# A two-block network on one core: 512 KB weight blocks fetched as two transfers of 64 rows

## The reference, cut to what matters

```python
proj = x @ w_in                                         # first layer: 2048 -> 3136
q = (_rmsnorm(c_q, q_norm) @ w_qb)                      # 512 -> 3072
kv = (_rmsnorm(c_kv, kv_norm) @ w_kvb)                  # 512 -> 4096
return (attn * jax.nn.silu(z)) @ w_out                  # 2048 -> 2048
...
proj = x @ w_in                                         # second layer: 2048 -> 8208
return (hcell * jax.nn.silu(z)) @ w_out                 # 2048 -> 2048
...
mod = c_act @ w_ada[l] + b_ada[l]                       # 2048 -> 12288, one row
proj = h @ w_in[l]                                      # second block: 2048 -> 8704
merged = jax.nn.sigmoid(ga) * (ya @ w_oa[l]) + jax.nn.sigmoid(gb) * (yb @ w_ob[l])
x = x + g1 * (merged @ w_out[l])
ff = (jax.nn.silu(h2 @ w_ffn_gate[l]) * (h2 @ w_ffn_up[l])) @ w_ffn_down[l]
```

## Time and profile before

| | |
|---|---|
| median of 3 runs | 2185.49 us |
| the profiled execution | 2186.84 us |
| its span | 2185.2 us |
| mean granted TensorE clock | 0.998 |
| TensorE busy | 2158.7 us |
| DVE busy | 1522.9 us |
| ScalarE busy | 1025.5 us |
| POOL busy | 311.0 us |
| moved by DMA | 522.69 MB, mean 239 GB/s |

### The profile page before, as it was taken

One profiled execution on the slowest core, in us unless ns is written; L12 is line 12 of the kernel. 1 busy time (PEld: TensorE's weight loads), 2 busy tenths in 40 slices (PEclk: granted clock), 3 DMA queues, 4 the chain that ended last, 5 costly groups with the idle time before them and its releaser, 6 DMA issues.

```text
span 2185.2 us, 30129 instructions
## 1 busy us (share of the span) xinstructions
PE 2158.7 (99%) x10030; PEld 1798.1 (82%) x10030; DVE 1522.9 (70%) x2065; ACT 1025.5 (47%) x1255; POOL 311.0 (14%) x580
## 2 busy tenths in 40 slices
PE   9999999999999999999999999999999999999998
PEld 8898888777888887887888888888888888888886
DVE  6766668788677978597876768775666666554544
ACT  5445544356445446434555444454444444444433
POOL 2101111221110010701111211111111111000000
PEclk9999999999999999999999999999999999999999
DMA  8887577897987684969766887757888887775564
GB/s 294 246 221 254 174 266 246 245 301 233 302 278 208 188 306 143 268 222 297 255 190 198 295 268 239 242 205 251 262 259 277 266 262 240 223 231 186 191 196 139
DMA packets 206444, 522.69 MB, mean 239 GB/s; under 512 B 33104, under 2 KB 60400, under 8 KB 205424
## 3 DMA queue, kind: packets, MB, share of 16 engines
q1 hardware_dynamic: 166256, 394.10, 56.7%
q0 software_dynamic: 39776, 126.41, 18.1%
q10 hardware_dynamic: 288, 0.52, 0.1%
HBM read 507.82 MB, written 13.16 MB: 238 GB/s over the span
## 4 chain that ended last, share of the span: by engine, by line
PE 89%; DVE 4%; DMA 3%; ACT 2%; issue 1%; SPq 0%; DVEq 0%; ACTq 0%
PE ps L2424 81%; PE ps L2468 2%; DMA ada_raw<-in_w_ada_dram 1%; DVE lo L1360 1%; DVE acc_s L1372 1%; ACT hi L771 1%; DMA raw<-in_ml_w_in_dram 1%; PE ps L2521 1%; PE ps L2894 1%; PE ps L2883 1%; PE ps L2781 0%; DMA raw<-in_w_in_dram 0%; DVE conv_tmp L1854 0%; PE ps L2614 0%; PE ps L2615 0%
## 5 line engine op out<-in xcount | busy, mean ns | idle before, releaser
L1360 DVE TENSOR_TENSOR lo<-raw,hi 128x1024 fp32r<-128x1024 f32 x731 | 889.9, 1222 | 547.5 <-ACT hi L771 544.6
L771 ACT CAST hi<-raw 128x1024 fp32r<-128x1024 f32 x731 | 765.4, 1051 | 991.1 <-PE ps L2424 808.4
L2424 PE MATMUL ps<-hi,XH 128*128 128x512 f32 x2196 | 686.8, 393 | 9.6 <-DVE lo L1360 7.4
L2424 PE MATMUL ps<-lo,XH 128*128 128x512 f32 x2196 | 680.1, 390 | 0.0
L2424 PE MATMUL ps<-hi,XL 128*128 128x512 f32 x2196 | 679.5, 389 | 0.0
L2424 PEld LDWEIGHTS ps<-hi,XH 128*128 128x128 f32 x2196 | 408.8, 188 | 97.0 <-DVE lo L1360 12.5
L2424 PEld LDWEIGHTS ps<-lo,XH 128*128 128x128 f32 x2196 | 412.7, 188 | 86.7
L2424 PEld LDWEIGHTS ps<-hi,XL 128*128 128x128 f32 x2196 | 412.5, 188 | 86.6
L643 POOL DMA_DIRECT2D ada_raw<-in_w_ada_dram x224 | 120.3, 537 | 788.1 <-DVE acc_s L1372 512.0
L1372 DVE SCALAR_TENSOR_TENSOR acc_s<-ada_raw,c_act,acc_s 128x512 f32<-128x512 f32 x256 | 191.1, 746 | 34.0 <-DMA ada_raw<-in_w_ada_dram 32.8
L665 POOL DMA_DIRECT2D ada_raw<-in_w_ada_dram x160 | 86.4, 541 | 346.5 <-DVE acc_s L1372 194.9
(11 more groups left out here) (396 smaller groups left out, 1695.5 us busy)
## 6 DMA issues: line engine op xcount, KB each, us to landing
ada_raw<-in_w_ada_dram POOLq DMA_DIRECT2D x384, 256.0 KB, 5.0
raw<-in_w_in_dram SPq DMA_DIRECT2D x136, 512.0 KB, 4.7
raw<-in_ml_w_in_dram SPq DMA_DIRECT2D x128, 512.0 KB, 4.7
raw<-in_w_gate_dram SPq DMA_DIRECT2D x176, 256.0 KB, 3.0
raw<-in_w_up_dram SPq DMA_DIRECT2D x176, 256.0 KB, 3.5
raw<-in_w_down_dram SPq DMA_DIRECT2D x88, 512.0 KB, 4.4
raw<-in_mla_w_in_dram SPq DMA_DIRECT2D x47, 512.0 KB, 5.1
raw<-in_mla_w_out_dram SPq DMA_DIRECT2D x32, 512.0 KB, 4.9
```

Source lines behind the costliest of these rows:

```text
L771: nc.scalar.copy(hi[:, j, :], raw[:, j, :]).then_inc(hi_ready, 1)
L1360: nc.vector.tensor_tensor(lo[:, j, :], raw[:, j, :], hi[:, j, :].bitcast(F32), ALU.subtract) \
L2424: ins = mm(ps[:, o:o + HALF], x, w[:, b % RING, c0:c0 + HALF], start=first, stop=(k == n_rows - 1 and x is xl), skip_group_check=True)
```

## The change

From the second projection on, every transfer of a 512 KB block is issued as two, rows 0 to 63 and rows 64 to 127, each 256 KB, into the same slot and onto the same semaphore. The first 16 blocks and the gate and up blocks stay as they are. All blocks behind the first 16 now count two transfers, and the wait targets follow.

```diff
@@ landed
-            two = max(0, min(n + 1, B_DOWN) - B_FFN)
-            two = (two + RING - 1 - j) // RING if two > 0 else 0
-            return 16 * (n // RING + 1 + two)
+            return 16 * (n // RING + 1 + max(0, n // RING + 1 - KD // RING))
@@ stream
                         sp.wait_ge(lo_ready, n0 + RING * g + j - RING + 1)
-                        sp.dma_start(dst, src).then_inc(w_landed[j], 16)
+                        for half in (slice(0, P // 2), slice(P // 2, P)):
+                            sp.dma_start(dst[half], src[half]).then_inc(w_landed[j], 16)
@@ blocks
                     sp.wait_ge(lo_ready, n0 + b - RING + 1)
-                    sp.dma_start(*plain(w, c0)(b, b % RING)).then_inc(w_landed[b % RING], 16)
+                    dst, src = plain(w, c0)(b, b % RING)
+                    for half in (slice(0, P // 2), slice(P // 2, P)):
+                        sp.dma_start(dst[half], src[half]).then_inc(w_landed[b % RING], 16)
@@ rest
-                        hi_block(RING * g + (n0 + j), j, 16 * g + c0)
+                        hi_block(RING * g + (n0 + j), j, 32 * g + c0)
```

## The result

The change makes the kernel slower: 2344.47 us median of six runs (2341.09 to 2350.51) against 2184.93 us beside it, a ratio of 1.0727 with a 95% interval of 1.0715 to 1.0739. That is 159.5 us more. The forecast was 2237 us with a range up to 2305; the sign was right and so was the cause (each transfer writes one side of the partitions), but the 50 us of the sum are a third of what came.

A forecast was written before the change was run, and what follows sets the result against it. TensorE was taken as the bound, with DMA near a limit in the fullest stages. Halves at 218 GB/s lose 50 us over the listed stretches: 2186.84 + 50 = 2237 us, range 2183 to 2305.

The forecast's parts named there:

- the sum: Over six stretches, weight bytes at 218 GB/s, all others at 406, excess over each stretch's length lost: together 50 us.
- What bounds it: Whole kernel: TensorE, busy 2158.7 of 2185.2 us, is the bound; only 26.5 us of idle time could be won.
- Issues and waits cost nothing: SP's two issues per block (0.67 of 2.72 us) and ScalarE's wait for 32 increments cost nothing.
- The rate of a half: Weight transfers to 64 partitions go at 218 GB/s, the mean of four regroup stretches; all other traffic at 406.
- the six stretches: Windows 294-354, 403-549, 549-633, 958-1052, 1217-1440 and 1929-2163 us (down projection, no cost); together 50 us lost.
- The stages not listed have room: Stages outside the sum give more time to a block or have less traffic beside it, so no loss.
- The path of the loss: In new stalls `raw` lands late, then `hi`, `lo`, TensorE wait; `ada` accumulations and `ada_raw` loads follow; no size given.
- The clock: TensorE's clock drops after idle time: five to ten drops of 1.7 us, counted in "Slower by more".
- Slower by more: Also the deeper rival: halves at 190 GB/s or less, plus clock drops; some 2330 us, chance 0.14.
- No difference: Regroups slow from their scratch source, or engines out of step; halves at about 400 GB/s, 2186 us, chance 0.21.
- faster: Split blocks land earlier; half a microsecond off each of ten late blocks is 5 us: 2182 us, chance 0.07.
- The signs: 549 to 633 us: 3.1 us per block, 250 to 270 GB/s, landings 3 us later; down projection share over 0.9.

The follow-up runs named there:

- regroup run: The kernel before with each regroup's four loads over all 128 partitions, a quarter of the columns each: 2180.07 us against 2186.13, ratio 0.9972.

## Why the prediction was right or wrong

**What bounds it.** Right. TensorE was the bound with next to nothing to win, the stages near 300 GB/s were near a limit, and the change pushed them over it.

**Issues and waits cost nothing.** Right within 3 to 6 us where blocks are on time, by the runs with even and odd rows and with columns, where the same number of transfers came to 1.0027 and 1.0011. One issue of 64 rows takes SP 468 ns, though, and not the 333 of a whole block, so a block costs it 0.94 us and not 0.67. And where blocks are late, the idle time that was to cover this is gone: SP's issues are 2% of the chain of the changed kernel, some 37 us if its pieces are added up, where they were under 1 us. How much of that is net loss was not separated.

**The rate of a half, taken at 218 GB/s, and all other traffic at 406.** The direction was right, and the nearest rows were of the right kind, as the regroup run shows. For the 32-block stage split alone the size held: 220 GB/s in the terms of the sum, and 12.7 us where the sum had 14.5. In the change, with split stages on both sides, the same stage comes to 205 GB/s and lost 18.3. The sum is steep there, since a block has 2.72 us and asks for 193 GB/s: by the prediction's own working the six stretches lose 50 us at 218 and 82 at 205. They lost 11.4 (306.3 to 362.9 before), 19.8, 18.3, 16.6, 29.8 (1217.3 to 1453.0 before) and 0 (down projection), 96 us in all. So this term was mis-sized by a factor of two, of which the lower rate explains two thirds.

The packet times show what was wrong in its form. The sum slowed the weights alone and left everything else at 406 GB/s. In the 32-block stage `ada_raw` went at 258 and the halves at 237; in the run with even and odd rows, with as many and as large transfers, `ada_raw` went at 369 (8.28 MB in 26.7% of 84 us). A confined transfer thus holds up its neighbours nearly as much as it is slowed itself. Nor were the rows behind 218 a rate of confined transfers beside weights: in 427 to 430 and 152 to 156 us nearly all bytes were those of POOL's queue, regroup loads and `ada_raw`; in 484 to 488 and 984 to 989 weights of 128 rows were about half.

The Trainium skill's rule (SBUF — State Buffer, "Door 1: The DMA port swizzle") spoke against the change, and the runs agree with the rule. Its 196 GB/s gave an estimated 107 us for those stretches, nearer to the 96 measured than my 50. The prediction calls the regroup rows within a few per cent of that figure; they lie 7 to 17% above it, and the halves' packet times of 223 to 263 GB/s lie 14 to 34% above. So the figure did well as a term of this sum, but the halves are nowhere seen to run at it.

**The stages not listed have room.** This is the step that failed: "they have room" on the average was taken for "no loss". The rest of the span's 154.2 us, 58 us, lies in them: 15.6 in the mLSTM output projection, 13.3 between 850 and 958 us (now 941.5 to 1062.8), 7.5 in the query, key and value stage, 7.3 in the first convolution inputs (362.9 to 402.8 before). In two of them, the mLSTM output projection and the first convolution inputs, SP puts 512 KB row loads between the blocks, and an average over the stage hides them. In the convolution inputs TensorE was busy all of the 39.9 us before, with the engines 81% busy. In the change a block behind the row loads landed 13.7 us after its issue, while the ring covers four blocks of work, 10.9 us, and TensorE was idle for 4.8 us of 47.2. Splitting the mLSTM output projection alone cost all of its 15 us, and splitting its first 12 blocks nothing clear of the noise. For the 13.3 us between 850 and 958 us and the 7.5 us of the query, key and value stage, the cause stays open.

**The path of the loss.** The prediction has `raw` as what is late, and `ada_raw` only behind a late `lo`. Landings of `raw` are the larger part. But `ada_raw` was late by itself, and DVE waited for it ahead of a `lo` (79.6 us against 32.8). The sum had no term for this.

**The clock.** I gave it to the deeper rival. The mean granted clock fell from 0.998 to 0.984. It was at 0.50 in twelve stretches of 3.4 to 10.2 us, 68 us together, where the kernel before had one of 3.4. In the 5 us ahead of each of the twelve, TensorE was busy for 0.5 to 3.0 us only. One of them:

```profile
190.00:195.40 5.40, 1.64 (x8) 1.02 (x6) 3.65 (x4) 1.34 (x2) 0.55 (x2) 1.00 1.03 247
195.50:202.30 6.80, 3.49 (x10) 3.03 (x11) 2.38 (x7) 4.15 (x4) 1.07 (x2) 0.50 1.03 254
```

At 0.50, 1.2 GHz, it stayed for 6.8 us here, as the earlier trace rows have it for 3.4. In full-speed time that is an estimated 37.4 us (0.016 of 2339.4) against 4.4 before, 33 us more, and it may explain most of the 48 us of added busy time. The 33 us bound from above what the clock can have cost by itself: where the next block is late anyway, a slower TensorE costs nothing. What part of them reached the end was not separated.

**The rivals.** "Slower by more" came nearest: 2330 us with a chance of 0.14, from a rate of 190 GB/s and the clock. Its time was right to 0.6%, its reason only in part, so the hit is mostly luck: in the terms of the sum the rate was not 190 but 205 in the clearest stage, the down projection lost nothing where it had 6.4 us, and stages that the sum had left out did the rest. "No difference" and "faster" are excluded by the measured time. The reason given for the first, the scratch tensor, is excluded by the regroup run; that given for the second, earlier landing, by the column halves, which did land earlier and gained nothing.

**The signs.** In the 32-block stage a block took 3.21 us (3.1 forecast) at a share of 1.01 and 246 GB/s (250 to 270 forecast). The median landing of `raw` there grew by 2.7 us, from 5.5 to 8.2 (3 or more forecast). The waits of `hi` for `raw` became large, and the gate and up stage kept its pace. The down projection was to show a share over 0.9; it showed 0.75 with no time lost. The prediction meant that share to test the rate of a half by itself, and by it a half costs 1.22 times the packet time of half a block, far from twice. Beside `ada_raw` it was 1.38 times, so the price of a half depends on what flows with it. Why it does stayed open.

## What to carry to other kernels

Let each transfer into SBUF span partitions on both sides of 64; if it must be cut, cut by columns or take every second row, which here cost 0.1% and 0.3% where two halves of the rows cost 7.3%. Before you trust a margin of DMA rate, don't average over a stage: look for the bursts in it (row loads, regroups) and ask if the depth of the ring covers one. Price the neighbours too: what slows one stream on shared engines slowed the other here (327 to 237 GB/s and 342 to 258). And close to saturation 6% of a rate (205 for 218 GB/s) moved the sum from 50 us to 82: there a range has to follow the rate, not the sum.

## What the runs showed of the hardware

- Even and odd partitions, 64 rows in each transfer, go as fast as 128 rows (302 GB/s at a share of 0.90 and 0.92 in the 32-block stage, 304 at 0.92 before); it is not the number of rows but which partitions they go to.
- Only the destination counts: the source in halves or in even and odd rows gave 2344.47 and 2344.26 us.
- Traffic of 128 partitions beside confined traffic suffers with it: landings of `ada_raw` went from a median of 5.0 to 7.2 us, its packet times in the 32-block stage from 342 to 258 GB/s, and three quarters of the loss went when it was cut.
- In the 32-block stage an issue of 64 rows took SP 468 ns (475 for even or odd rows), one of 128 rows 333 and one of 32 rows 316.
- Four pieces of 32 rows that alternate sides did better than two of 64, 1.0507 against 1.0727, against what more issues would suggest. Size and order were not told apart.
